# Running the entry of phase 2 inside the last inverse block of phase 1, without a full stop between the two

## The reference

```
h    = rmsnorm(x) * (1 + sc1) + sh1
proj = h @ w_in                       # hg_q, hg_f, hg_i, hg_g | mb_z, mb_xbc, mb_dt | rw_p
o_hg = rmsnorm(hgrn2_chunked(q, (1-lb)*sigmoid(-f), i, logf)) * silu(hg_g)
xbc  = silu(conv4(mb_xbc) + b);  dt = softplus(mb_dt + bias);  A = -exp(A_log)
y_mb = rmsnorm((ssd_chunked(x, dt, A, B, C) + D*x) * silu(mb_z))
o_rw = groupnorm(rwkv7_scan(r, w, k, v, kk, a)) + bonus, times g
x    = x + g1 * (concat(o_hg, y_mb, o_rw) @ w_out)
x    = x + g2 * ((silu(h2 @ w_gate) * (h2 @ w_up)) @ w_down)     # h2: second modulated norm
y    = rmsnorm(x);  new states of all three mixers are outputs too
```

## Time and profile before

| | |
|---|---|
| median of 3 runs | 1989.53 us (1986.57 to 1996.15) |
| profiled execution | 1990.94 us, span 1989.2 us |
| TensorE (PE) busy | 1666.2 us, 84% of the span |
| VectorE (DVE) busy | 977.0 us, 49% |
| ScalarE (ACT) busy | 589.8 us, 30% |
| GpSimd (POOL) busy | 253.4 us, 13% |
| mean granted TensorE clock | 0.891 |

### The profile page before, as it was taken

One profiled execution on the slowest core, in us unless ns is written; L12 is line 12 of the kernel. 1 busy time (PEld: TensorE's weight loads), 2 busy tenths in 40 slices (PEclk: granted clock), 3 DMA queues, 4 the chain that ended last, 5 costly groups with the idle time before them and its releaser, 6 DMA issues.

```text
span 1989.2 us, 31929 instructions
## 1 busy us (share of the span) xinstructions
PE 1666.2 (84%) x13471; PEld 1509.8 (76%) x13471; DVE 977.0 (49%) x2105; ACT 589.8 (30%) x1055; POOL 253.4 (13%) x331
## 2 busy tenths in 40 slices
PE   4898888887888537578888887999969999999995
PEld 2898777776877423246677777988869999999995
DVE  5405436665643256756666734545653333433335
ACT  2324223312322132123433434333342212222222
POOL 3501001110100022103233341000000000000000
PEclk9899889888988757668888989999989999999998
DMA  8110001010100045432121232433312131221311
GB/s 298 38 53 22 22 17 38 29 40 26 58 30 29 11 159 170 146 97 58 55 62 54 70 116 86 122 106 104 124 54 82 56 97 56 74 86 55 98 47 54
DMA packets 199013, 149.22 MB, mean 75 GB/s; under 512 B 6447, under 2 KB 187168, under 8 KB 197592
## 3 DMA queue, kind: packets, MB, share of 16 engines
q1 hardware_dynamic: 188482, 120.67, 20.1%
q0 software_dynamic: 7440, 23.27, 3.4%
q10 hardware_dynamic: 2950, 3.24, 0.5%
HBM read 134.03 MB, written 13.18 MB: 74 GB/s over the span
## 4 chain that ended last, share of the span: by engine, by line
PE 68%; DVE 18%; ACT 6%; DMA 4%; issue 3%; POOL 0%; SPq 0%; POOLq 0%; DVEq 0%; ACTq 0%
PE bank L1240 17%; PE bank L1241 17%; PE bank L1242 17%; PE bank L1179 3%; DMA RAW<-in_w_ada 1%; PE bank L1592 1%; PE bank L1591 1%; ACT WHI L1764 1%; PE bank L1427 1%; PE bank L1428 1%; PE bank L1376 1%; PE bank L1383 1%; PE bank L1438 1%; PE bank L1385 1%; PE bank L1248 1%
## 5 line engine op out<-in xcount | busy, mean ns | idle before, releaser
L1240 PE MATMUL bank<-HBH,WHI 128*128 128x328 f32 (+1 forms) x832 | 261.7, 315 | 14.8 <-DVE HBL L2319 10.1
L2202 DVE TENSOR_TENSOR WLO<-RAW,WHI 128x1024 fp32r<-128x1024 f32 (+4 forms) x149 | 152.3, 1025 | 237.5 <-ACT WHI L1764 236.9
L1764 ACT CAST WHI<-RAW 128x1024 fp32r<-128x1024 f32 (+4 forms) x210 | 187.9, 898 | 250.8 <-PE bank L1242 244.5
L1241 PE MATMUL bank<-HBL,WHI 128*128 128x328 f32 (+1 forms) x832 | 260.2, 313 | 0.0
L1242 PE MATMUL bank<-HBH,WLO 128*128 128x328 f32 (+1 forms) x832 | 259.4, 312 | 0.0
L1240 PE MATMUL bank<-HHI,WHI 128*128 128x344 f32 x624 | 212.8, 341 | 11.8 <-DVE HLO L2415 5.9
L1241 PE MATMUL bank<-HLO,WHI 128*128 128x344 f32 x624 | 205.3, 329 | 0.0
L1242 PE MATMUL bank<-HHI,WLO 128*128 128x344 f32 x624 | 204.7, 328 | 0.0
L1003 POOL TENSOR_TENSOR WLO<-RAW,WHI 128x1024 fp32r<-128x1024 f32 (+1 forms) x61 | 130.5, 2143 | 502.5 <-ACT WHI L1764 502.5
L1240 PEld LDWEIGHTS bank<-HBH,WHI 128*128 128x128 f32 x832 | 157.7, 190 | 16.4 <-issue 16.2
L1242 PEld LDWEIGHTS bank<-HBH,WLO 128*128 128x128 f32 x832 | 157.9, 190 | 0.0
(11 more groups left out here) (554 smaller groups left out, 3152.6 us busy)
## 6 DMA issues: line engine op xcount, KB each, us to landing
RAW<-in_w_gate SPq DMA_DIRECT2D x44, 512.0 KB, 3.9
RAW<-in_w_up SPq DMA_DIRECT2D x44, 512.0 KB, 3.9
RAW<-in_w_ada SPq DMA_DIRECT2D x32, 512.0 KB, 4.6
RAW<-in_w_in SPq DMA_DIRECT2D x26, 512.0 KB, 3.8
ADAW<-in_w_ada SPq DMA_DIRECT2D x8, 1024.0 KB, 19.9
RAW<-in_w_out SPq DMA_DIRECT2D x16, 512.0 KB, 4.2
RAW<-in_w_down SPq DMA_DIRECT2D x32, 256.0 KB, 2.7
RAW<-in_w_down SPq DMA_DIRECT2D x16, 384.0 KB, 3.5
```

Of the source, the lines that this page charges most:

```text
L1240: mm(bank[:, 0:w], whi[:, k, :], hi_k, start=(k == 0), stop=False)
L1241: mm(bank[:, 0:w], whi[:, k, :], lo_k, start=False, stop=False)
L1764: a.copy(w_split(i)[0][:, 0:nk, :], RAW[u % NRAW][:, 0:nk, :]).then_inc(w_hi, 1)
L2202: v.tensor_tensor(wlo[:, 0:nk, :], RAW[u % NRAW][:, 0:nk, :], whi[:, 0:nk, :].bitcast(F32), ALU.subtract).then_inc(w_lo, 1)
```

## The change

- **Dense work in phase 1.** `BEHIND` gets one quantum behind `seq0` too, so that the 54 quanta stand behind blocks 0 to 6. The silu items come as soon as their quantum was brought out, in the order in which the quanta come (z, then hg's gate).
- **Entry in block 7.** A table, `ENTRY`, puts phase 2's entry behind the items of block 7: loads of `XB` and `HB` and hg's memsets, the copies of `rw_final` in five pieces through one bank (`fin` 0 to 4), the six Sigmoids and products (`xs`), `pre` in four pieces, and all of hg block 0 up to `hg_o`.
- **No stop.** `end_phase` between the phases is gone, `rw_final` too. `XB` moves over `HHI`/`HLO`, mb's buffers move to where `XB` was; `PSG` and `FST` lie over phase 1's weight buffers. TensorE's first ada quantum waits for `fin` 4.
- **hg one block ahead.** With `HGA = 1`, iteration b runs hg block b + 1 and mb block b. Items of blocks beyond the last are left out, but the fill behind them is kept.

```diff
-        BEHIND = {'turn': 1, 'lin': 1, 'gates': 1, 'inv4': 1, 'post': 1, 'decay': 2}
+        BEHIND = {'turn': 1, 'lin': 1, 'gates': 1, 'inv4': 1, 'seq0': 1, 'post': 1, 'decay': 2}
...
+        ENTRY = {
+            ('rw_turn', 7): [('entry', 0)],
+            ('rw_inv1', 7): [('fin', 0)],
+            ('rw_inv2', 7): [('hg_logits', 0)],
+            ('rw_inv3', 7): [('hg_gate', 0), ('fin', 1)],
+            ('rw_inv4', 7): [('xs', 0), ('xs', 1), ('xs', 2)],
+            ('rw_inv5', 7): [('hg_levels', 0), ('xs', 3), ('xs', 4), ('xs', 5)],
+            ('rw_fold', 7): [('pre', 0), ('fin', 2)],
+            ('rw_seq0', 7): [('hg_att', 0), ('pre', 1)],
+            ('rw_seq1', 7): [('hg_state', 0), ('pre', 2), ('fin', 3)],
+            ('rw_post', 7): [('hg_o', 0), ('pre', 3)]}
...
-            if item[0] in ('rw_lin', 'rw_inv2', 'rw_lora', 'rw_inv3') and silu and (
-                    item[1] >= (4 if item[0] in ('rw_lin', 'rw_lora') else 3)):
+            if item[0] in ('rw_lin', 'rw_inv2', 'rw_lora', 'rw_inv3') and silu and silu[0] + 1 < brought[0]:
                 PLAN1.append(('silu', silu.pop(0)))
-        assert not silu
-        fill1(len(left))
-        PLAN1.append(('ev', QP1 - 1))
-        PLAN1.append(('rw_final', 0))
-
-        PLAN2 = [('pre', 0), ('hg_logits', 0), ('mb_turn', 0), ('hg_gate', 0), ('hg_levels', 0)]
...
+            PLAN1 += ENTRY.get(item, [])
+        assert not silu and not left
+
+        PLAN2 = [('fin', 4), ('hg_logits', 1), ('mb_turn', 0), ('hg_sq', 0), ('hg_gate', 1), ('hg_out', 0), ('hg_levels', 1)]
...
+            h = b + HGA
+            items = [('hg_att', h), ('hg_state', h), ('mb_decay', b), ('hg_o', h), ('hg_logits', h + 1), ('mb_prod', b),
+                     ('hg_sq', h), ('hg_gate', h + 1), ('mb_turn', b + 1), ('mb_sq', b), ('hg_out', h),
+                     ('hg_levels', h + 1), ('mb_out', b), ('hg_x', b)]
             for item in items:
-                if item[1] == NB or (item[0] == 'hg_x' and b > 2):
+                if item[0] == 'hg_x' and b > 2:
                     continue
-                PLAN2.append(item)
+                if item[1] < NB:
+                    PLAN2.append(item)
...
+            def entry():
+
+                pool.wait_ge(dense_done, QP1)
+                pool.wait_ge(acc_out, 16 * 18)
+                for k in range(2):
+                    pool.wait_ge(stg_out[k], 16 * 9)
+                load_hg(0)
+                for t in range(6):
+                    pool.dma_start(XB[t][:, :], xbd[t]).then_inc(mb_loaded[t], 16)
+                load_hg(1)
...
                 if kind == 'ada':
+                    if q == QP1:
+                        pe.wait_ge(fin_dve, 5)
...
                     pe.wait_ge(hgf_dve, step(HGF_DVE, 'factors', b))
-                    if b:
-                        pe.wait_ge(mb_act, step(MB_ACT, 'rs', b - 1))
+                    if b == 0:
+                        pe.wait_ge(evac['act'], EVN[QP1 - 1])
+                    else:
+                        pe.wait_ge(hg_act, step(HG_ACT, 'rs', b - 1))
+                    if b > HGA:
+                        pe.wait_ge(mb_act, step(MB_ACT, 'rs', b - HGA - 1))
...
-            end_phase(pe, 1)
```

More of the change, by code:

```diff
@@ L388, in kernel_program @@
         HR = r2.t("HR", [P, 2, BLK])
[L389 to L402, removed]
+        XB = [r2.t(f"XB{t}", [P, T]) for t in range(6)]
         DT = r2.t("DT", [P, 9, 8])
@@ L422, in kernel_program @@
         SW1 = Region(smt_at, w1.at).t("SW1", [P, 1024])
+        w1x = Region(h_end + 4096, w1.at)
+        PSG = [w1x.t(f"PSG{i}", [P, T]) for i in range(2)]
+        FST = w1x.t("FST", [64, 2, P])
         r2b = Region(mix_end, hi)
@@ L1687, in mix_final @@
                 last.then_inc(fin_pe, 1)
+            for what, arg in PLAN1 + PLAN2[:1]:
+                if what == 'mm':
+                    dense(arg)
+                elif what == 'dt':
+                    rw_init()
+                    dt_proj()
+                elif what[:3] == 'rw_':
+                    rw(what[3:], arg)
+                elif what[:3] == 'hg_':
+                    hg(what[3:], arg)
+                elif what == 'rws0':
+                    rws0()
+                elif what == 'pre' and arg == 1:
+                    pre()
+                elif what == 'fin':
+                    fin(arg)
             for what, arg in PLAN2:
-                if what == 'pre':
-                    pre()
-                elif what == 'mm':
+                if what == 'mm':
                     dense(arg)
@@ L2149, in sample @@
                     ssq_scale(NS, S, SRM, 256).then_inc(ms_act, 1)
+            for what, arg in PLAN1:
+                if what == 'split':
+                    split_hi(arg)
+                elif what == 'ev':
+                    bring_out(arg)
+                elif what == 'silu':
+                    silu_gate(arg)
+                elif what == 'xs':
+                    silu_xb(arg)
+                elif what == 'pre':
+                    pre(arg)
+                elif what[:3] == 'rw_':
+                    rw(what[3:], arg)
+                elif what[:3] == 'hg_':
+                    hg(what[3:], arg)
+            tables(LN_EXP)
             for what, arg in PLAN2:
-                if what == 'pre':
-                    pre()
-                elif what == 'adt':
+                if what == 'adt':
                     ada_act(arg)
@@ L2965, in sample @@
                     mb_out(SYS, SRM, slice(SEQ, T), ms_dve)
+            for what, arg in PLAN1 + PLAN2[:1]:
+                if what == 'split':
+                    if LO_BY[arg] == 'dve':
+                        split_lo(arg)
+                elif what == 'ev':
+                    bring_out(arg)
+                elif what == 'silu':
+                    silu_gate(arg)
+                elif what == 'xs':
+                    silu_xb(arg)
+                elif what == 'dt':
+                    read_states()
+                elif what == 'pre':
+                    pre(arg)
+                elif what == 'fin':
+                    fin(arg)
+                elif what[:3] == 'rw_':
+                    rw(what[3:], arg)
+                elif what[:3] == 'hg_':
+                    hg(what[3:], arg)
             for what, arg in PLAN2:
-                if what == 'pre':
-                    pre()
-                elif what == 'adt':
+                if what == 'adt':
                     modulate(arg)
```

305 lines of the change are left out of this document (146 added, 159 removed).

## The result

The changed kernel takes 1999.4 us (median of eleven runs, 1996.0 to 2005.5) against 1991.7 for the kernel before on the same chips: a ratio of 1.0043, 95% interval 1.0026 to 1.0061. That is inside the 0.5% that I called no change, but reliably a little slower, where I had forecast 1979, 0.6% faster. The profiled execution has a span of 2000.8 us, against 1989.2.

What follows compares the result with a forecast made beforehand. TensorE's in-order queue was taken to set the pace in the inverse blocks, and latency in the 44.3 us stop. The terms 7 - 7 + 32 - 30 - 14 gave -12 us: 1979 us, its own range 1970 to 1988.

Steps and rivals of the forecast that it cites:

- (a): Blocks 0 to 5 gain a quantum each behind `seq0`: +1.2 us each, +7 in all, bounds -5 and +37.
- second rival: The added quantum behind `seq0` stays slow and lifts no clock: +6.2 us a block, 2009 us; chance 0.20.
- credit of 4.0: Blocks 0 to 5: if the clock stays up, the sequence, sums and dense start behind `post` shrink, -4.0 us a block.
- if it falls again before `post`: Blocks 0 to 5: case where the clock falls again after the added quantum, +2.1 us a block.
- 5 us either way: Moved convolutions and gates' Sigmoids put at nothing, with 5 us either way where they meet.
- (b): Block 6 loses five quanta, -13 us, but runs partly at the low clock, +6: sum -7, bounds -13 and -4.
- (c): Block 7 without its dense quantum and with entry work between its steps: +8.5 low clock, +25 entry, +32 in all.
- (d): The stop between the phases shrinks to 14 us from 44.4: -30 us.
- (e): Phase 2's last iterations, with one hg block fewer and more fills in waits: -14 us.
- The stop's idle only moves: Rival: block 7's steps cost 7 us more, or phase 2's last iteration gives only -7: 1986 to 1993; chance 0.16.
- the clock stays up without dense work: Rival: the clock stays high in blocks 0 to 5 and block 7: -38 us, 1953, half of it 1966; chance 0.18.
- The quantum behind `seq0` runs slow and lifts nothing: Rival for blocks 0 to 5: +6.2 us a block instead of +1.2, 30 more, 2009 us; chance 0.20.

Runs made afterwards that it cites:

- e2: The changed kernel with its eighth quantum behind the second inverse step `inv2` instead of behind the first sequence step: 1997.1 us, ratio 1.0020 to the kernel before.
- e4: The changed kernel with the weight splits of the new slot moved behind the second sequence step: 1993.9 us, ratio 1.0004 to the kernel before.
- e3: The kernel before with only the slot behind the first sequence step added, stop and Sigmoids as they were: 2023.8 us, ratio 1.0167.
- e8: e1 with the gates' 18 Sigmoids back in blocks 3 to 7, as in the kernel before: 1977.1 us, ratio 0.9941 to the kernel before.
- e6: e1 with all entry work except the loads put behind block 7's last product: 1988.1 us, ratio 0.9978 to the kernel before.
- e11: The changed kernel, eight quanta per block, with hg not one block ahead of mb: 1990.0 us, ratio 0.9977 to the kernel before.
- e7: e1, seven quanta per block, with hg not one block ahead of mb: 1970.4 us, ratio 0.9892 to the kernel before.
- e10: e7 with quanta behind both sequence steps, none behind `inv4`, one behind `decay`, one more ahead of block 0: 1964.1 us, ratio 0.9839 to the kernel before.
- e1: The changed kernel with seven quanta per block instead of eight, none behind the first sequence step: 1975.8 us, ratio 0.9927 to the kernel before.

## Why the prediction was wrong

**(a) is the step that failed:** "Net +0.6 ... I take +1.2 each", for the eighth quantum. It measured 33.8 / 6 = 5.6 us a block, over the 4.6 at which my second rival decides. Its first half, 5.3 us less 0.7 of waiting, is just what block 1 shows. What failed is the credit of 4.0 for a sequence, sums and dense start that would run high: only the second sequence step did, 1.8 us, and the dense work behind `post` starts low for 3.5 us instead of 2.7 after the second fall. Three things make up the 33.8:

- *The quantum itself, 23 us, 3.8 a block.* From the fold to the next block, block 1 grew by 3.1 us, and the six by 3 to 5 each once the split below is taken off. My "if it falls again before `post`" (+2.1) was the right picture with too small a price, since it still let the sums run high. e2 shows that another place is no better: in the high part the quantum costs 3.8 with nothing hidden. TensorE is busy 334 of 398 us in these blocks, and the waits that are left, as the 0.47 us for `PS`, lie in a chain from engine to engine that a quantum beside them doesn't shorten. In the earlier trace rows I had read that the queue sets the pace, and then priced a quantum below its own duration.
- *The split beside VectorE, 2 us in two blocks.* Not in my list at all: I moved the convolutions with their quanta and forgot the weight splits. The trace of e4 shows it: moved away, 4.42 us are 2.40 again.
- *Inverse steps that meet convolutions.* Up to the last inverse step, blocks 0 to 5 take 6.9 us more in all (block 2 alone 5.3). The rows of block 2 above show how: convolution, late `Y`, a wait of 2.42 us and a clock that falls. e3 has the same in block 2 with the Sigmoids at their old places, and e8 clears the Sigmoids. It was "5 us either way" in my text; no run isolates it.

**(b)** held: -8.0 against -7. The reason was right too: in the changed kernel TensorE waits 7.47 us for `VZ` ahead of block 7, so the quanta behind block 6 had lain in part where it had to wait anyway. With (a) it says what the redistribution is: six quanta at about 5 us each, for five in block 6 at 1.8.

**(c)** was 5 too long, +27.1 against +32. Its two largest pieces came as priced:

```profile
693.83 0.49 PE L1405 MATMUL bank<-PS,Y 64*64 64x64 f32 x4 [5.57 <-ACT PS L2023]
...
709.53 0.47 PE L1449 MATMUL bank<-AR,ST 64*64 64x64 f32 x2 [0.69 <-DVE UV L2664]
...
723.94 0.47 PE L1449 MATMUL bank<-AR,ST 64*64 64x64 f32 x2 [0.69 <-DVE UV L2664]
```

The wait for `PS` at `inv4` is 5.6 us instead of 0.5 (+5.1, forecast +4.9), and the second sequence step starts 14.4 us after the first, where it was 5.4 (+9.0, forecast +9.2). The stage ran mostly at the low clock as I said (mean 0.57), which is worth about 7 by e3, not 8.5. But my reading that only dense quanta lift the clock was wrong. Block 7 has none, and from 681.3 to 691.3 it ran at 1.00, after TensorE had been busy for 10.8 of 11.5 us with small products and transposes. The kernel before had shown it already: 1.00 from 689.8 to 693.1, behind the transposes of the stop. By e6, the entry work would have cost 9 to 12 us more behind the block than between its steps.

**(d)** and **(e)** held: -30.8 against -30, -11.8 against -14. (e) also came where I put it: from the first products of the last `mb_turn` to the end it is 872.7 us instead of 886.8. What I did not draw from my own numbers is that hg one block ahead is a loss: I had 9.2 + 4.3 us for it in block 7 and some 10 of the 14 behind it, against 14 gained. The traces of e11 and the changed kernel show 22 against 11, and e7 and e11 measured 5.5 and 9.4 less without it.

**The rivals.** "The stop's idle only moves" and "the clock stays up without dense work" are out: (c) to (e) came near the forecast, and block 7 ran low but for some 10 us. "The quantum behind `seq0` runs slow and lifts nothing" had the sign right and the picture half. The quantum lifts the clock for some 7 us and still costs its own time. Its +6.2 a block is near the measured 5.6 by chance: the slot gave 3.8 of them, the split and the inverse steps, which it did not name, the rest. The Trainium skill, TensorE: Matmul & The Clock Gate, section "HAM oscillation — how this bites in real kernels", says that short bursts of matmuls between waits pay the clock's transition each time. That was nearer here than my net: in block 1 the clock falls twice instead of once, in blocks 0 to 5 fifteen times instead of eight. (Blocks 3 and 4 had two falls already before, so "one fall per block" was too simple.) e10 shows that waits of this length need not bring the clock down: 0.69 and 1.05 us between dense quanta left it at 1.00.

## What to carry to other kernels

Where an in-order TensorE queue is as full as here (334 of 398 us), price work that is added to it at its full duration, less only waits that the trace shows at that very place. Let a credit for "the clock will then stay up" in only once a trace shows the level all the way to the next dense work. Look also at what comes with the work on the other engines, here splits and convolutions. Before spreading dense work evenly, find the stretch in which it is nearly free (1.8 us a quantum in block 6, against about 5) and leave it there. A change with several parts should be cut apart on the chip: this one measured +0.4%, holds a version worth -0.7% (e1), and with hg back in step and dense work on both sides of the sequence came to -1.6% (e10).

## What the runs showed of the hardware

- The granted clock fell twice in a block: after a wait of 2.40 us, and again some 7 us after it had risen (0.92 from 220.0, 0.95 up to 227.5, 0.50 behind), with no wait over 1.04 us between; yet with a second dense quantum behind the sequence step (e10) it held at 1.00 over waits of 0.69 and 1.05.
- It rose without a dense quantum in block 7 of the changed kernel, at about 681.3, after 10.8 us of small products and transposes within 11.5.
- A VectorE product of 128x256 with both inputs in SBUF took 2.44 us beside a GpSimd subtraction of 2.58, against 0.42 alone, and a VectorE operation with one tensor and its factors in SBUF (`ACC`) 2.19 beside one of 2.35; operations that read a bank were not slowed.
- Executions of one kernel differ with the mean granted clock: of the ten of e1, the slowest took 1989.0 us at 0.882 and the fastest 1969.1 at 0.893. A single profile can so sit 13 us off the median, as that of e1 does, and blocks with the same list took 404.6 us in it and 400.2 and 401.0 in e6 and e7.
